# A fused two-block kernel on one core: another order of work in its first stage

## The chip, the cores and the metric

The kernel runs on one core of one Trainium2 chip. The metric is the device time of one execution in microseconds (us). Before the change it is 1601.06 us, the median of three runs (1599.04 to 1601.58).

## The reference

The input x has 512 rows of 1024 channels. Two blocks are computed in float32, cut here to what matters.

```python
def gated_deltanet_mixer(h, w_in, conv_w, a_log, dt_bias, o_gain, w_out):   # first mixer; h = rms_norm(x, a_norm)
    proj = h @ w_in                       # 4096 channels q,k,v; 2048 channels z; 16 channels "ab"
    qkv, z, ab = jnp.split(proj, [A_CONV_CH, A_CONV_CH + A_V_W], axis=-1)
    qkv = jax.nn.silu(causal_depthwise_conv(qkv, conv_w))                    # 4 taps
    q, k, v = ...                         # 8 heads; q and k are l2-normed
    beta = jax.nn.sigmoid(b_logit)
    g = -jnp.exp(a_log) * jax.nn.softplus(a_logit + dt_bias)                 # the gates, from the 16 channels
    o = chunk_gated_delta_rule(q, k, v, g, beta)                             # per head: a triangular solve, then a recurrence
    o = rms_norm(o, o_gain) * jax.nn.silu(z)
    return o @ w_out
```

After it come an attention with a sliding window, a second block with a pooling and a stick-breaking attention, an MLP and a gated embedding. The change touches nothing in those.

## The kernel before, in words

Everything is laid out with channels on the 128 partitions and the 512 rows of x along the free axis. The weights come as 214 blocks of 128x1024 (512 KB), each good for one group: 8 pieces, one for each 128 of the 1024 inner channels. A block passes from `wraw` (four buffers, loaded by the SP queue) to a high part `wh` (ACT, L1274) and a low part `wl` (DVE, L1867), both in the reduced float32 type; x is split in the same way into `XR[k]` and `XR[8+k]`. A piece is three matmuls of 512 columns, high x high, high x low and low x high (`mm3`), so a group is 24 matmuls into one PSUM bank. `walk` gives the order of a group's steps: OPEN (the blocks ahead are split), MM (one piece) with a STEP behind it, CLOSE (the eviction of a finished group) with a STEP. `Pace` says how many blocks are split ahead at each OPEN.

Each engine has its own program with the same parts, and `follow` runs them all in one order that is written by hand. `weave(g, order, parts, beside)` takes a plan such as "g10 g9 g17": it runs the next step of the named part (g, p, q, r) and then so many steps of the products. The engines keep to that order, each waiting on semaphores for what it needs.

The first stage goes so. `begin`: SP loads the eight tiles of x with the first weight blocks between them; ACT's queue loads gains, k1 (constants, among them the matrix of ones and the identity), wab (the gates' weights) and alog; POOL's queue loads the masks. ACT makes the high part of each tile of x times the gain (L1366), DVE the low part (L2064); then ACT squares the tiles (L1370) and DVE adds them up into `sqa` (L2070), clears `cin` (L2071) and splits the gates' weights (L2073). `products(1)` are the four groups of head 0, the first three side by side (`walk` with wide=3: for each piece k of x, one piece of each group), four groups of head 1 and six groups z. 24 steps of it run first. Then `rms_x` (ACT: logarithm and exponential of the sum of squares, L1379 and L1381, which give the row factor `rb_a`), 11 steps more, and then the gates with plan "a0": PE sums the squares over partitions with the matrix of ones and does the gates' product (24 matmuls with 16 weight columns); behind ten steps it transposes the scaled result (L898); behind nine more it does the product of gg with the triangle, for the running sum. DVE and ACT do the gates' short chain between (L2088 to L2102, L1394 to L1412). As the row factor is the same for all channels, it is applied when a group is evicted: for a head group DVE's multiplication into `cin` (L1917), then ACT's first tap of the convolution (L1302) and DVE's three others (L1903, the function `tap`). A z group has one eviction (L1922).

Plan "a1" then weaves `prep(0)` (part p) with the rest of `products(1)`. Its PE steps are the sum of k's squares (ks), G, kk, qk, the transposes kT, v0 and v1, all through one PSUM bank, so each waits until DVE or ACT has emptied it. Beside them DVE computes Dm, AT, qkT, kg and kd and the sums dc, then 15 shuffles of rows; POOL selects, masks, and inverts the 16x16 diagonal blocks in 15 turns of two instructions (L2611, L2613); DVE then writes U (L2183) and turns it into Tm (L2189). Plan "a2" weaves `prep(1)` (p), `levels(0)` (q), which starts with PE's product of Tm, and `recur(0)` (r) with the products of head 2 and z6.

Of the kernel before, what the change touches and what calls it, by code (L numbers as in the profile page):

```python
# [127 lines left out]
class Ring:  # L128


    def __init__(self, banks):
        self.use(banks)
# [118 lines left out]
def weave(g, order, parts, beside):  # L251
# [11 lines left out]

PLAN = {
    "a0": plan("g10 g9 g17"),
    "a1": plan("p5 p8 p2 p1 p2 p3 p10 p6 p6 p9 p6 p11 p14 p8"),
    "a2": plan("p2 p0 p0 q1 p2 q3 q1 p0 q5 q2 q0 p0 q2 p0 q3 r0 p1 r3 r1 r0 r1 p0 r1 r1 r4 p0 p1 r0 r2 p2 p5 p0 r1"),
# [20 lines left out]
def follow(p):  # L288
# [30 lines left out]
    def products(i):  # L319
        return chain(*(gemm(what, groups_of(what, h), 3 if (what, h) == ("head", 0) else 0, h) for what, h in PRODUCTS[i]))  # L320
# [3 lines left out]
    for _ in range(24):  # L324
        next(g)
    do("rms_x")
    for _ in range(11):
        next(g)
    banks(EARLY)
    weave(g, PLAN["a0"], {"g": part("gates")}, p.get("tap"))  # L330
    out = gemm("ao", pair_groups("wao", 8), 3, None, 2)
# [298 lines left out]
class Signals:  # L630


    def __init__(self, nc, ctx):
# [22 lines left out]

        self.gate_p, self.gate_a, self.gate_v = new("gate_pe"), new("gate_act"), new("gate_dve")
# [121 lines left out]
def tensor_program(e, m, s):  # L779
    p = {}  # L780
    ring = Ring(WIDE)
# [103 lines left out]
    def gates():  # L885
        e.wait_ge(s.k1, 16)
        e.wait_ge(s.xacc, 9)
        mm(m.banks[2][:], m.ones, m.sqa_a[:]).then_inc(s.nsum, 1)
        clear[2] = [(s.nln, 1)]
        e.wait_ge(s.gate_v, 1)  # L890
        for k, (xh, xl) in enumerate(m.pieces("head")):
            ins = mm3(m.banks[7][0:16, :], m.wabh[:, k, :], m.wabl[:, k, :], xh, xl, k == 0, k == 7)
        ins.then_inc(s.gate_p, 1)
        clear[7] = [(s.gate_v, 2)]
        yield
# [5 lines left out]
        clear[3] = [(s.gate_v, 3)]  # L901
        yield
# [351 lines left out]
def scalar_program(e, m, s):  # L1254
    p = {}
    ring, pace = Ring(WIDE), Pace()
# [96 lines left out]
    def begin():  # L1353
        e.dma_start(m.gains[:], m.d["gains"]).then_inc(s.gains, 16)
        e.dma_start(m.k1[:], m.d["k_k1"]).then_inc(s.k1, 16)
        e.dma_start(m.wab[:], m.d["wab"]).then_inc(s.wab, 16)
        e.dma_start(m.al[:], m.d["alog"]).then_inc(s.alog, 16)
        tables()
        for k in range(8):
            x = m.XF[:, 16 + k, :]  # L1360
            if k in (1, 2, 4):
                split(pace.upto(k // 2 + 1))
            e.wait_ge(s.x[k], 16)
            if k == 0:
                e.wait_ge(s.gains, 16)
            e.activation(m.XR[:, k, :], x, ACT.Copy, scale=m.gain("a_norm", k)).then_inc(s.xhi, 1)  # L1366
        for k in range(8):
            if k >= 2:
                e.wait_ge(s.xacc, k)
            e.activation(m.sqt_a[:, k % 2, :], m.XF[:, 16 + k, :], ACT.Square).then_inc(s.xsq, 1)  # L1370
        e.wait_ge(s.wab, 16)
        e.activation(m.wabh[:], m.wab[:], ACT.Copy).then_inc(s.gate_a, 1)
        passed["gate"] += 1
# [42 lines left out]
    def prep(h):  # L1416
# [43 lines left out]
        if h < 2:  # L1460
            e.wait_ge(s.xacc, 9)
        else:
            e.wait_ge(s.rec_v, REC_V * (h - 2) + 4)
# [383 lines left out]
def vector_program(e, m, s):  # L1847
    p = {}
    ring, pace = Ring(WIDE), Pace()
# [57 lines left out]
    def evac_head(n, bank, i, h):  # L1907
# [4 lines left out]
        if c == 0:  # L1912
            e.wait_ge(s.nrb, 1)
            e.wait_ge(s.xacc, 10)
# [144 lines left out]
    def begin():  # L2059
        for k in range(8):  # L2060
            if k in (1, 2, 4):
                split(pace.upto(k // 2 + 1))
# [3 lines left out]
        e.memset(m.sqa_a[:], 0.0).then_inc(s.xacc, 1)  # L2066
        for k in range(8):
            e.wait_ge(s.xsq, k + 1)
            e.wait_ge(s.xacc, k + 1)
            e.tensor_tensor(m.sqa_a[:], m.sqa_a[:], m.sqt_a[:, k % 2, :], ALU.add).then_inc(s.xacc, 1)  # L2070
        e.memset(m.cin[:], 0.0).then_inc(s.xacc, 1)  # L2071
        e.wait_ge(s.gate_a, 1)
        e.tensor_tensor(m.wabl[:], m.wab[:], m.wabh[:].bitcast(F), ALU.subtract).then_inc(s.gate_v, 1)  # L2073
        passed["gate"] += 1
# [447 lines left out]
def pool_program(e, m, s):  # L2522
# [13 lines left out]
    def begin():  # L2536
        e.dma_start(m.masks[:], m.d["k_masks"]).then_inc(s.masks, 16)
# [125 lines left out]
def sync_program(e, m, s):  # L2663
# [38 lines left out]
    def begin():  # L2702
# [4 lines left out]
        for k in (1, 2, 4):  # L2707
# [186 lines left out]
```

## Time and profile before

| | before |
|---|---|
| median of three runs | 1601.06 us |
| the profiled execution's own time | 1599.54 us |
| its span, first to last instruction | 1597.7 us |
| PE busy (matmuls) | 1548.9 us, 97% |
| DVE, ACT, POOL busy | 885.0, 747.5, 223.5 us |
| mean granted clock of TensorE | 0.995 |
| moved by DMA | 127.22 MB, mean 80 GB/s |

The profile is of one execution. PE is busy nearly all the time, so its idle time is the first thing to look for: the page shows the span in 40 slices of 40 us, one digit a slice, and PE's first two digits are 6 and 8, the others 9 save the last. The timeline is then read for the first 130 us, with the releaser of each wait in brackets behind a row.

### The profile page before, as it was taken

The numbers are of one execution on the slowest core, as the hardware profiler recorded it, in microseconds if no ns is written. First come the engines' busy times: TensorE is split into PE (matmuls) and PEld (weight loads), VectorE is DVE, ScalarE is ACT, GpSimd is POOL, SyncE is SP. The second block draws the span as 40 slices with busy tenths as digits, with TensorE's granted clock in tenths as the row PEclk, the third lists the DMA queues.
The fourth block names the chain that finished last, engine by engine and source line by source line (L and its number), as shares of the span: only waits on it lengthen the run. The fifth ranks groups of instructions, "written<-read, shape, count | busy, mean of one in ns | idle before, by whom it ended". The sixth has DMA issues, their size and how long they took to land.

```text
span 1597.7 us, 20673 instructions
## 1 busy us (share of the span) xinstructions
PE 1548.9 (97%) x7686; PEld 1228.5 (77%) x7686; DVE 885.0 (55%) x1633; ACT 747.5 (47%) x1293; POOL 223.5 (14%) x451
## 2 busy tenths in 40 slices
PE   6899999999999999999999999999999999999998
PEld 5688888888878767777777887666678888888876
DVE  4666777776666355555556435444366243443466
ACT  4453555544553346665567415555446232322333
POOL 1034224433323001221122000000000000000000
PEclk9999999999999999999999999999999999999999
DMA  4221111111114232222222232112122323232321
GB/s 185 80 84 49 54 58 63 53 54 59 48 53 150 81 106 81 85 67 80 67 86 67 80 105 75 53 53 66 53 80 80 106 93 106 93 105 87 98 81 65
DMA packets 40163, 127.22 MB, mean 80 GB/s; under 512 B 4576, under 2 KB 9104, under 8 KB 40064
## 3 DMA queue, kind: packets, MB, share of 16 engines
q1 hardware_dynamic: 38112, 121.65, 23.7%
q0 software_dynamic: 1040, 3.27, 0.6%
q8 instruction: 62, 1.02, 0.3%
q10 hardware_dynamic: 912, 0.99, 0.2%
q14 instruction: 37, 0.30, 0.1%
HBM read 122.69 MB, written 2.15 MB: 78 GB/s over the span
## 4 chain that ended last, share of the span: by engine, by line
PE 83%; DVE 7%; ACT 6%; issue 2%; DMA 1%; POOL 1%; SPq 0%; ACTq 0%; DVEq 0%; POOLq 0%
PE ps L792 81%; ACT L L1674 3%; DVE L L2353 1%; DVE wl L1867 1%; PE ps L1127 1%; DVE qkv L1903 1%; PE ps L919 1%; ACT wh L1274 1%; DMA wraw<-in_wa 1%; ACT L L1626 1%; DVE cin L1917 0%; DVE h L2488 0%; ACT xm L1809 0%; POOL masks L2611 0%; ACT qkv L1302 0%
## 5 line engine op out<-in xcount | busy, mean ns | idle before, releaser
L792 PE MATMUL ps<-xr,wh 128*128 128x512 f32 x2752 | 891.9, 405 | 15.1 <-DVE wl L1867 13.7
L792 PEld LDWEIGHTS ps<-xr,wh 128*128 128x128 f32 x2752 | 506.2, 189 | 144.6 <-issue 36.3
L792 PE MATMUL ps<-xr,wl 128*128 128x512 f32 x1376 | 540.0, 392 | 0.0
L1867 DVE TENSOR_TENSOR wl<-wraw,wh 128x1024 fp32r<-128x1024 f32 x214 | 262.0, 1230 | 157.7 <-ACT wh L1274 155.5
L792 PEld LDWEIGHTS ps<-xr,wl 128*128 128x128 f32 x1376 | 259.6, 189 | 56.2
L1274 ACT ACTIVATE wh<-wraw 128x1024 fp32r<-128x1024 f32 x214 | 221.8, 1049 | 81.9 <-PE ps L792 78.2
L792 PE MATMUL ps<-xm,wh 128*128 128x512 f32 x640 | 200.1, 394 | 6.7 <-DVE xm L2473 3.7
L792 PEld LDWEIGHTS ps<-xm,wh 128*128 128x128 f32 x640 | 120.3, 189 | 35.3 <-DVE xm L2473 5.0
L792 PE MATMUL ps<-xm,wl 128*128 128x512 f32 x320 | 125.1, 391 | 0.0
L2643 POOL TENSOR_SCALAR L<-L,m 128x256 f32<-128x256 f32 (+1 forms) x128 | 62.4, 510 | 315.5 <-DVE m L2368 315.5
L1903 DVE SCALAR_TENSOR_TENSOR qkv<-cin,gains,qkv 128x512 f32<-128x512 f32 x96 | 82.1, 855 | 11.1 <-ACT qkv L1302 10.3
L792 PEld LDWEIGHTS ps<-xm,wl 128*128 128x128 f32 x320 | 60.5, 189 | 12.6
L1674 ACT ACTIVATE L<-L,m 128x256 f32<-128x256 f32 (+1 forms) x128 | 59.9, 469 | 18.5 <-DVE m L2359 18.5
L1326 ACT ACTIVATE sqt<-sqt 128x512 f32<-128x512 f32 x32 | 20.2, 632 | 100.7 <-DVE sqt L2019 100.6
L1572 ACT ACTIVATE sqt<-h 128x512 f32<-128x512 f32 x24 | 14.9, 629 | 100.8 <-DVE h L1932 53.9
L2353 DVE CUSTOM_DVE_ANT_0 L<-ps,bias,sinks 128x256 f32<-128x256 f32 (+1 forms) x128 | 50.1, 447 | 13.9 <-PE ps L792 13.9
L2611 POOL TENSOR_TENSOR masks<-nb,uc 128x60 f32<-128x60 f32 (+14 forms) x120 | 44.1, 368 | 87.8 <-DVE nb L2173 72.1
L2038 DVE TENSOR_TENSOR mo<-ps,mo 128x512 f32<-128x512 f32 x24 | 16.6, 692 | 66.9 <-PE ps L792 66.9
L1694 ACT ACTIVATE pT<-ps 128x512 f32<-128x512 f32 x32 | 19.1, 597 | 71.1 <-PE ps L1127 71.1
L1302 ACT ACTIVATE qkv<-cin,gains 128x512 f32<-128x512 f32 x32 | 23.0, 723 | 50.1 <-DVE cin L1917 49.7
L2019 DVE SCALAR_TENSOR_TENSOR sqt<-ps,rb 128x512 f32<-128x512 f32 x32 | 22.0, 691 | 41.0 <-PE ps L792 36.0
L2613 POOL TENSOR_TENSOR uc<-uc,masks 128x60 f32<-128x60 f32 (+14 forms) x120 | 41.5, 346 | 9.4
(258 smaller groups left out, 1769.0 us busy)
## 6 DMA issues: line engine op xcount, KB each, us to landing
wraw<-in_wa SPq DMA_DIRECT2D x48, 512.0 KB, 3.7
wraw<-in_wb SPq DMA_DIRECT2D x32, 512.0 KB, 3.9
wraw<-in_wu SPq DMA_DIRECT2D x32, 512.0 KB, 3.7
wraw<-in_wd SPq DMA_DIRECT2D x32, 512.0 KB, 3.7
wraw<-in_wao SPq DMA_DIRECT2D x16, 512.0 KB, 3.7
wraw<-in_wbo SPq DMA_DIRECT2D x16, 512.0 KB, 4.0
wraw<-in_wc SPq DMA_DIRECT2D x16, 512.0 KB, 3.7
bias<-rel_rows SPq DMA_DIRECT2D x16, 256.0 KB, 3.9
```

The source lines that it names most:

```text
L792: return e.matmul(out, w, x, start=start, stop=stop, skip_group_check=True)
L1274: e.activation(m.wh[:, i % N_SPLIT, :], m.raw[:, i % N_RAW, :], ACT.Copy).then_inc(s.whi, 1)
L1302: e.activation(m.qkv[:, h % 2, n, :], m.cin[:, b, 3:515], ACT.Copy, scale=m.convw[:, 3, ch:ch + 1]).then_inc(s.conv0, 1)
L1326: e.activation(f, f, ACT.Square).then_inc(s.sq, 1)
L1674: e.activation(x, x, ACT.Exp, bias=m.nmx[:, c, u:u + 1], accum_out=m.den[:, c, u:u + 1]).then_inc(s.ex, 1)
L1867: e.tensor_tensor(m.wl[:, i % N_SPLIT, :], m.raw[:, i % N_RAW, :], m.wh[:, i % N_SPLIT, :].bitcast(F), ALU.subtract).then_inc(s.wlo, 1)
L1903: e.scalar_tensor_tensor(out=dst, in0=m.cin[:, c % 2, w:w + 512], scalar=m.convw[:, w, ch:ch + 1], in1=dst, op0=ALU.mult, op1=ALU.add).the ...
L2019: e.scalar_tensor_tensor(out=m.sqt[:, n % 2, :], in0=bank[:], scalar=0.0, in1=m.rb[:], op0=ALU.max, op1=ALU.mult).then_inc(s.relu, 1)
L2353: e.tensor_tensor_reduce(out=m.L[:, c, ee, n, lo:], in0=m.banks[4 + ee][:, 256 * (n % 2) + lo:256 * (n % 2) + 256], in1=m.bias[:, c, ee, lo:],
L2611: did(e.tensor_tensor(part, nb[:, :, r + 1:], m.uc[:, :, r:r + 1].to_broadcast([128, 4, w]), ALU.mult))
L2613: did(e.tensor_tensor(m.uc[:, :, r + 1:], m.uc[:, :, r + 1:], part, ALU.add))
L2643: e.tensor_scalar(x, x, m.den[:, c, 2 * n + ee:2 * n + ee + 1], 1.0, ALU.mult, ALU.mult).then_inc(s.pr, 1)
```

## The change

- Loads: k1 and alog are issued by ACT behind x's piece 4 (k counts from 0) and the split of block 2. The masks are issued by POOL once ACT has made five high parts of x.
- Order in `begin`: the splits of weight blocks 0, 1 and 2 stand behind x's pieces 0, 2 and 4 (before: ahead of pieces 1, 2 and 4, so behind 0, 1 and 3). The gates' weights are split at piece 0 instead of at the end. The sum of squares begins with a copy of the first square, not with a memset and an addition. `cin` is cleared by POOL at the very start.
- Head 0's first three groups still run side by side, but each now is two pieces behind the one before it (SKEW_X = 2), so there are 12 turns with one to three pieces each.
- The gates' product goes ahead of each of the first eight turns, a piece of three matmuls each time (`gates_x`). The sum of squares and the row factor (`rms_x`) come at turn 10. Plan "a0" goes from "g10 g9 g17" to "g52 g20 g14": the transposes come at once, the gates' chain on ACT and DVE 52 steps later, the product of gg 20 steps after that; the open taps are then all done (`flush`). Plans "a1" and "a2" are changed with it.
- PE begins with nine products of 128 columns on the cleared `cin`, whose result nobody reads.
- The order of the PSUM banks is (6, 0, 1, 4, 5) from the start.

```diff
     def __init__(self, banks):
-        self.use(banks)
+        self.banks, self.turn = banks, 0
     def use(self, banks):
...
+
+SKEW_X, RMS_AT, N_ZERO = 2, 10, 9
 PLAN = {
-    "a0": plan("g10 g9 g17"),
-    "a1": plan("p5 p8 p2 p1 p2 p3 p10 p6 p6 p9 p6 p11 p14 p8"),
-    "a2": plan("p2 p0 p0 q1 p2 q3 q1 p0 q5 q2 q0 p0 q2 p0 q3 r0 p1 r3 r1 r0 r1 p0 r1 r1 r4 p0 p1 r0 r2 p2 p5 p0 r1"),
+    "a0": plan("g52 g20 g14"),
+    "a1": plan("p1 p2 p2 p0 p2 p1 p1 p0 p1 p16 p14 p20 p10 p30"),
+    "a2": plan("p1 p4 p2 q0 p2 q4 q1 q2 q0 p0 q2 p0 q2 p0 q3 r0 p1 r0 r1 p0 r0 r2 r1 p0 r2 r0 r0 p4 r2 p0 p2 p0 r6"),
     "a8": plan("p0 q1 p2 q3 q1 q0 p0 q0 p3 q0 p0 q0 p0 q0 p1 r1 r0 r1 r0 p0 r0 p2 p0 r0 p0 r0 p2 r5 p0 r1 p0 r2 r1"),
...
     def products(i):
-        return chain(*(gemm(what, groups_of(what, h), 3 if (what, h) == ("head", 0) else 0, h) for what, h in PRODUCTS[i]))
+        return chain(*(gemm(what, groups_of(what, h), *((3, h, SKEW_X) if (what, h) == ("head", 0) else (0, h)))
+                       for what, h in PRODUCTS[i]))
...
     g = products(1)
-    for _ in range(24):
-        next(g)
-    do("rms_x")
-    for _ in range(11):
-        next(g)
-    banks(EARLY)
+    skew = SKEW_X
+    for t in range(8 + 2 * skew):
+        if t < 8:
+            do("gates_x", t)
+        drain(take(g, sum(0 <= t - skew * n < 8 for n in range(3))))
+        if t == RMS_AT:
+            do("rms_x")
     weave(g, PLAN["a0"], {"g": part("gates")}, p.get("tap"))
+    flush()
     out = gemm("ao", pair_groups("wao", 8), 3, None, 2)
...
+        self.cin = new("cin_cleared")
+
         self.gate_p, self.gate_a, self.gate_v = new("gate_pe"), new("gate_act"), new("gate_dve")
...
     p = {}
-    ring = Ring(WIDE)
+    ring = Ring(EARLY)
     p["banks"] = ring.use
...
     @part
-    def gates():
+    def begin():
+
+        e.wait_ge(s.cin, 1)
+        for _ in range(N_ZERO):
+            mm(m.banks[2][:, 0:128], m.cin[:, 0, 0:128], m.cin[:, 1, 0:128])
+
+    @part
+    def gates_x(k):
+
+        xh, xl = m.pieces("head")[k]
+        if k == 0:
+            e.wait_ge(s.gate_v, 1)
+        e.wait_ge(s.xlo, k + 1)
+        ins = mm3(m.banks[7][0:16, :], m.wabh[:, k, :], m.wabl[:, k, :], xh, xl, k == 0, k == 7)
+        if k == 7:
+            ins.then_inc(s.gate_p, 1)
+            clear[7] = [(s.gate_v, 2)]
+
+    @part
+    def rms_x():
         e.wait_ge(s.k1, 16)
-        e.wait_ge(s.xacc, 9)
+        e.wait_ge(s.xacc, 8)
         mm(m.banks[2][:], m.ones, m.sqa_a[:]).then_inc(s.nsum, 1)
         clear[2] = [(s.nln, 1)]
-        e.wait_ge(s.gate_v, 1)
-        for k, (xh, xl) in enumerate(m.pieces("head")):
-            ins = mm3(m.banks[7][0:16, :], m.wabh[:, k, :], m.wabl[:, k, :], xh, xl, k == 0, k == 7)
-        ins.then_inc(s.gate_p, 1)
-        clear[7] = [(s.gate_v, 2)]
-        yield
+
+    @part
+    def gates():
         e.wait_ge(s.gate_v, 2)
...
         clear[3] = [(s.gate_v, 3)]
+        yield
         yield
...
     p = {}
-    ring, pace = Ring(WIDE), Pace()
+    ring, pace = Ring(EARLY), Pace()
     p["banks"] = ring.use
...
     def begin():
         e.dma_start(m.gains[:], m.d["gains"]).then_inc(s.gains, 16)
-        e.dma_start(m.k1[:], m.d["k_k1"]).then_inc(s.k1, 16)
         e.dma_start(m.wab[:], m.d["wab"]).then_inc(s.wab, 16)
-        e.dma_start(m.al[:], m.d["alog"]).then_inc(s.alog, 16)
         tables()
         for k in range(8):
-            x = m.XF[:, 16 + k, :]
-            if k in (1, 2, 4):
-                split(pace.upto(k // 2 + 1))
             e.wait_ge(s.x[k], 16)
...
                 e.wait_ge(s.gains, 16)
-            e.activation(m.XR[:, k, :], x, ACT.Copy, scale=m.gain("a_norm", k)).then_inc(s.xhi, 1)
+            e.activation(m.XR[:, k, :], m.XF[:, 16 + k, :], ACT.Copy, scale=m.gain("a_norm", k)).then_inc(s.xhi, 1)
+            if k in (0, 2, 4):
+                split(pace.upto(k // 2 + 1))
+            if k == 0:
+                e.wait_ge(s.wab, 16)
+                e.activation(m.wabh[:], m.wab[:], ACT.Copy).then_inc(s.gate_a, 1)
+                passed["gate"] += 1
+            elif k == 4:
+                e.dma_start(m.k1[:], m.d["k_k1"]).then_inc(s.k1, 16)
+                e.dma_start(m.al[:], m.d["alog"]).then_inc(s.alog, 16)
         for k in range(8):
             if k >= 2:
-                e.wait_ge(s.xacc, k)
+                e.wait_ge(s.xacc, k - 1)
             e.activation(m.sqt_a[:, k % 2, :], m.XF[:, 16 + k, :], ACT.Square).then_inc(s.xsq, 1)
-        e.wait_ge(s.wab, 16)
-        e.activation(m.wabh[:], m.wab[:], ACT.Copy).then_inc(s.gate_a, 1)
-        passed["gate"] += 1
...
     def rms_x():
...
         if h < 2:
-            e.wait_ge(s.xacc, 9)
+            e.wait_ge(s.xacc, 8)
         else:
...
     p = {}
-    ring, pace = Ring(WIDE), Pace()
+    ring, pace = Ring(EARLY), Pace()
     p["banks"] = ring.use
...
             e.wait_ge(s.nrb, 1)
-            e.wait_ge(s.xacc, 10)
+            e.wait_ge(s.cin, 1)
         elif c >= 2:
...
     def begin():
         for k in range(8):
-            if k in (1, 2, 4):
-                split(pace.upto(k // 2 + 1))
             e.wait_ge(s.xhi, k + 1)
...
                                    in1=m.XR[:, k, :].bitcast(F), op0=ALU.mult, op1=ALU.subtract).then_inc(s.xlo, 1)
-        e.memset(m.sqa_a[:], 0.0).then_inc(s.xacc, 1)
+            if k in (0, 2, 4):
+                split(pace.upto(k // 2 + 1))
+            if k == 0:
+                e.wait_ge(s.gate_a, 1)
+                e.tensor_tensor(m.wabl[:], m.wab[:], m.wabh[:].bitcast(F), ALU.subtract).then_inc(s.gate_v, 1)
+                passed["gate"] += 1
         for k in range(8):
             e.wait_ge(s.xsq, k + 1)
-            e.wait_ge(s.xacc, k + 1)
-            e.tensor_tensor(m.sqa_a[:], m.sqa_a[:], m.sqt_a[:, k % 2, :], ALU.add).then_inc(s.xacc, 1)
-        e.memset(m.cin[:], 0.0).then_inc(s.xacc, 1)
-        e.wait_ge(s.gate_a, 1)
-        e.tensor_tensor(m.wabl[:], m.wab[:], m.wabh[:].bitcast(F), ALU.subtract).then_inc(s.gate_v, 1)
-        passed["gate"] += 1
+            if k == 0:
+                e.tensor_copy(m.sqa_a[:], m.sqt_a[:, 0, :]).then_inc(s.xacc, 1)
+            else:
+                e.wait_ge(s.xacc, k)
+                e.tensor_tensor(m.sqa_a[:], m.sqa_a[:], m.sqt_a[:, k % 2, :], ALU.add).then_inc(s.xacc, 1)
...
     def gates():
...
     def begin():
+        e.memset(m.cin[:], 0.0).then_inc(s.cin, 1)
+        e.wait_ge(s.xhi, 5)
         e.dma_start(m.masks[:], m.d["k_masks"]).then_inc(s.masks, 16)
...
                 load(k // 2 + 1)
-        for k in (1, 2, 4):
+        for k in (0, 2, 4):
             split(pace.upto(k // 2 + 1))
```

## Rows read from the trace of the kernel before

**Rows 1.** Waits of PE, 0 to 130 us: waiting <- releaser: total us, times, longest.

```profile
PE ps L792 <- DVE wl L1867: 12.4, 3, 9.0
```

**Rows 2.** Timeline of PE, 0 to 60 us: start, us, engine, line, operation, [idle before].

```profile
9.05 1.22 PE L792 MATMUL ps<-xr,wh 128*128 128x512 f32 x2 [9.05 <-DVE wl L1867]
...
13.09 1.22 PE L792 MATMUL ps<-xr,wh 128*128 128x512 f32 x2 [2.39 <-DVE wl L1867]
...
15.71 1.22 PE L792 MATMUL ps<-xr,wh 128*128 128x512 f32 x2 [0.98 <-DVE wl L1867]
...
19.50 0.63 PE L792 MATMUL ps<-xr,wh 128*128 128x512 f32 x2
...
37.21 0.62 PE L792 MATMUL ps<-xr,wh 128*128 128x512 f32 x2
```

**Rows 3.** Timeline of ACT and DVE, 0 to 60 us: the first pieces and the gates' weights.

```profile
4.10 0.72 ACT L1366 ACTIVATE xr<-xreg,gains 128x512 fp32r<-128x512 f32 x1 [0.18 <-DMA gains<-in_gains]
...
6.68 1.06 ACT L1274 ACTIVATE wh<-wraw 128x1024 fp32r<-128x1024 f32 x1 [1.86 <-DMA wraw<-in_wa]
...
7.77 1.23 DVE L1867 TENSOR_TENSOR wl<-wraw,wh 128x1024 fp32r<-128x1024 f32 x1 [2.16 <-ACT wh L1274]
...
24.43 0.30 ACT L1372 ACTIVATE wab<-wab 128x128 fp32r<-128x128 f32 x1
...
26.45 0.23 DVE L2073 TENSOR_TENSOR wab<-wab,wab 128x128 fp32r<-128x128 f32 x1
```

**Rows 4.** Windows (busy us by engine, PEclk, DMA share, GB/s), then DMA issues, 0 to 20.

```profile
0.00:10.00 10.00, 0.95 (x2) 0.84 (x3) 2.57 (x3) 3.78 (x4) 0.88 (x5) 1.00 0.83 304
...
masks<-in_k_masks POOLq DMA_DIRECT2D x1, 448.0 KB, 6.8
...
k<-in_k_k ACTq DMA_DIRECT2D x1, 420.0 KB, 6.5
```

**Rows 5.** Timeline, 20 to 60 us: the sum of squares, the factor, the gates' transposes.

```profile
37.90 1.02 PE L792 MATMUL ps<-sqa,k 128*128 128x512 f32 x2
...
39.74 0.63 ACT L1381 ACTIVATE rb<-rtmp 128x512 f32<-128x512 f32 x1
...
49.98 0.67 DVE L2088 TENSOR_TENSOR rtmp<-ps,rb 16x512 f32<-16x512 f32 x1
...
50.70 0.42 PE L898 MATMUL ps<-k,rtmp 16*128 16x16 f32 x4 [0.79 <-DVE rtmp L2088]
```

**Rows 6.** Timeline of DVE, 20 to 60 us: the weights' low part and two evictions.

```profile
48.83 1.23 DVE L1867 TENSOR_TENSOR wl<-wraw,wh 128x1024 fp32r<-128x1024 f32 x1 [1.74 <-ACT wh L1274]
...
52.99 0.69 DVE L1917 TENSOR_TENSOR cin<-ps,rb 128x512 f32<-128x512 f32 x1
...
58.99 0.69 DVE L1917 TENSOR_TENSOR cin<-ps,rb 128x512 f32<-128x512 f32 x1
```

**Rows 7.** Timeline of PE, 56 to 130 us: the wait for the gates and the products behind.

```profile
62.17 1.03 PE L792 MATMUL ps<-gg,k 128*128 128x32 f32 x4 [5.39 <-DVE gg L2102]
...
63.02 1.20 PE L792 MATMUL ps<-xr,wh 128*128 128x512 f32 x2
...
67.00 0.66 PE L792 MATMUL ps<-xr,wh 128*128 128x512 f32 x2
```

**Rows 8.** Timeline, 56 to 130 us, PE, DVE, POOL: head 0 from its norm to its levels.

```profile
76.83 1.10 PE L792 MATMUL ps<-rq,k 128*128 128x512 f32 x2 [0.76 <-ACT rq L1438]
...
95.24 0.68 DVE L2165 TENSOR_TENSOR kd<-ps,g 128x512 f32<-128x512 f32 x1
...
99.63 0.29 POOL L2611 TENSOR_TENSOR masks<-nb,uc 128x60 f32<-128x60 f32 x1 [7.59 <-DVE nb L2173]
...
113.03 0.21 POOL L2613 TENSOR_TENSOR uc<-uc,masks 128x4 f32<-128x4 f32 x1
...
116.30 0.71 DVE L2189 STREAM_TRANSPOSE Tm<-U 128x512 f32<-128x512 f32 x1
...
117.80 1.06 PE L792 MATMUL ps<-Tm,Mm 128*128 128x128 f32 x8
```


## The prediction

> **What bounds the kernel now.** I read the page first: PE is busy 97% of the span, and its low digits stand in the first slices. Then the waits of PE by stretch: between 0 and 130 us it waits 12.4 us for the weights' low parts in three pieces [rows 1], and further only for the four waits named below; the timeline shows no idle gap of PE between 77 and 260 us. So behind head 0's norm PE sets the pace, and any microsecond that PE gets back ahead of it, and doesn't lose again, comes off the end. The reader should make a ledger of what PE loses up to the first product of the levels (117.80 us) [rows 8]. A "piece" is three matmuls of 512 columns; at full pace 26 pieces run from 19.50 to 37.21 us, 0.681 us each [rows 2].
>
> The losses before: it starts at 9.05; it waits 2.39 and 0.98 for the second and third weight block; the first two lone pieces run at half pace (1.22 + 0.43, so 1.65 instead of 0.68: 1.94 together); from 15.71 to 19.50 three pieces take 3.79 instead of 2.04 (1.75) [rows 2]. It waits 0.79 for the gates' transposes [rows 5] and 5.39 for the gates (gg), behind which three pieces again run at half pace, 63.02 to 67.00, 3.98 instead of 2.04 (1.94) [rows 7]; and 0.76 for the squares of k [rows 8]. Sum 9.05 + 3.37 + 1.94 + 1.75 + 0.79 + 5.39 + 1.94 + 0.76 = **25.0 us**. The half pace is the 1.2 GHz level (512 columns in 0.43 us), though the window's granted clock reads 1.00 [rows 4]: here durations tell more than that column.
>
> **The start.** The DMAs are the limit: the window 0 to 10 has a DMA share of 0.83 at 304 GB/s, and in it land 448 KB of masks and 420 KB of k1 [rows 4], which go behind x. 868 KB at some 400 GB/s (the rate from 3 us on) are 2.2 us. x0's pass on ACT starts at 4.10 because of the table load and the gains [rows 3], and stays. Block 0 lands at 6.68 before; without k1 and masks ahead of it some 5.0. Then ACT's high part (1.06) ends 6.05, the gates' high part (0.30) 6.35, DVE's low part (1.23, from 6.05) 7.3, the gates' low part (0.23) **7.5** [rows 3]. There PE starts with the first gates product. New against before: the gates' product of each piece goes ahead of it, so PE has six pieces of work (7.5 to 11.6) before it asks for block 1, which is split by about 10.1, and block 2 is split by 12.8 when PE asks at 15. The skew of two pieces does that: no wait for blocks 1 and 2 (3.37 saved, and the lone pieces too). The gates' 24 products are not new work: they move from behind the sum. The squares go behind all of x: 5 us of ACT and 6 of DVE, done at about 21.5; the sum asks for them at 28.6, 7 us of cover. x's last low part comes at 14.8 instead of 18.3, asked for later still. k1 and alog now cost ACT two issues in mid stream (0.9 us, ahead of x5), which DVE, itself behind with low parts, hides; if x5 were late, PE would have 3 us to spare.
>
> **The products of zeros.** Nine f32 products of 128 columns, behind a memset of cin that goes to POOL. No row has either. A 512-column f32 product is 1.10 us at full pace [rows 8], so 0.28 for 128 columns, 0.55 at half: nine are 2.5 to 4.9 us. POOL starts about 1.3 and needs about a microsecond (DVE takes 0.92), so they end between 5 and 7.2, before 7.5: nothing in their own right. What they may give is the clock: the pace rose 3.8 us after 15.71 and 4.8 after 62.17 [rows 2, 7], and four microseconds of zeros are about that. I take full pace at 7.5 (idle gaps of 0.8 us left it at full, [rows 5, 8], one of 5.39 didn't, [rows 7]; the gap here is 0.5 to 2); the other end is 1.75 to 1.94 us. The Trainium skill, "TensorE: Matmul & The Clock Gate", Part 1, says that the chip watches how busy the array was, and that the number of slow matmuls differs between runs of one kernel; by that this term is not the same in all executions. No run here shows it for zeros.
>
> **The factor's wait.** From 7.5, 32 pieces and the sum (0.95) last until 30.25. The sum is issued at 28.6 with one piece behind it, then PE's transposes wait for the factor and the gates' scaling. Before: the sum is issued at 37.90, the factor done at 40.37, the scaling 0.67 on DVE, transposes 0.05 later [rows 5]: 3.25 us; so transposes at 31.85, and PE waits **1.6** (0.79 before).
>
> **The gates' wait.** The gg product now stands 72 steps behind the transposes (9 before), and its chain on ACT and DVE begins 52 steps behind them: 5.39 and the 1.94 of slow pieces behind it go, and nothing follows, since ACT and DVE need some 3 us and have 12.
>
> **Weight blocks in the first stage.** For the head groups the chain low part, three taps, eviction, first conv product on ACT, high part, low part is serial: evictions start 6.00 us apart (52.99, 58.99) [rows 6], while PE needs 8 x 0.681 = 5.45 per block. Before, the gates' wait paid for that. Now block 5 is split 9.7 us behind the factor (40.37 to 50.06) [rows 5, 6]: 31.1 + 9.7 = 40.8, block 10 five turns later at 70.8; PE asks for it at 32.2 + 7 x 5.47 = 70.4. Loss **0.4**; the earlier blocks are just in time. If PE started sooner, this chain would be late instead: it caps the gain.
>
> **Head 0 with less beside it.** 110 steps of the products now lie ahead of its norm instead of 71, so only 14 pieces are left beside it (49 before). PE: norm's sum at 83.4, then G, kk, qk, kT, v0, v1 through one bank with 3, 2, 1, 1, 1, 0 pieces between. G 86.4, kk 88.7, qk 90.4 and kT 92.1 wait 0.1 each at most. v0 waits for kd: kT ends 92.55, DVE has a low part (1.23) and kg, kd (0.68 each) [rows 6, 8] from 92.05: 94.65, PE there at 93.2: **1.4**. v1 waits for ACT's copy of v0: **0.65**. Then six pieces, head 1's norm sum, five pieces, and G of head 1 behind ACT's chain (two table loads, six silu and square passes, a weight block): about **0.55**. The levels wait for head 0's inversion on POOL: first shuffle 95.6. Before, POOL's steps ran from 99.63 to 113.24 (13.6 us, with a hole and three long ones beside DVE work), and DVE's two passes ended at 117.01 [rows 8]. With the shuffles in one go and DVE quiet I take 12 (ends: 10.9, 13.6) plus 1.5: 109.4. PE is there at 107.5: **1.9** (0.8 to 3.5).
>
> **The sum.** Losses after: 7.5 + 1.6 + 0.4 + 0.2 + 1.4 + 0.65 + 0.55 + 1.9 = 14.2. Gain 25.0 - 14.2 = 10.8. Cross-check by the levels' first product: before 117.80 with 114 pieces done, after 109.45 with 119 done: 117.80 + 3.4 - 109.45 = 11.7. I take 11.2. From there on nothing is changed but the order in head 1's stage, which I cost at nothing (bounds -1.5 and +2: PE doesn't wait between 118 and 260 now, so it can hardly gain). Against the profiled execution's 1599.54 that is 1588.3; the median of the runs is 1601.06, which gives 1589.9. I forecast **1589.0**.
>
> **The rivals.** (a) *The zeros don't raise the clock*, or it falls before 7.5: for it, no row shows f32 zeros at work and the gap up to 2 us; against it, the two times of rise. 1.75 to 1.94 more: 1591. (b) *The head 0 chain hides better than I wrote*: POOL in 10.9 us, PE's waits for kd and v0 shorter; up to 4 us less loss, 1585.5. Against it: kg, kd really stand behind a low part on DVE in both orders. (c) *The new orders expose more*: DVE stands in front of the inversion with head 2's weights and evictions queued behind it; only two blocks are split ahead. Waits of 3 to 6 us: 1594. (d) *Slower, one mechanism*: the chain from head 0's norm to the levels keeps the length that it has now, 76.83 to 117.80, 41 us [rows 8], since it is paced by engines and not by PE's order. PE has between the two only 21 pieces and some 7 us of f32 products, 21.4 us: it idles 19.6, and with 7.5 + 1.6 + 0.4 loses 29.1 against 25.0: 4 us slower, 1603.5. It decides from a chain of 37 us. Against it: 51 pieces of PE filled that chain, and the sum of its passes is 26 us. (e) *k1 and masks behind x don't speed block 0*, since the queues share the engines otherwise: start at 8.5 to 9, 1.0 to 1.5 more, 1590.3.
>
> **How the numbers follow.** The forecast with (e), 1587 to 1591: 0.55. (a) alone or with (e), 1591 to 1593: 0.14. (b) 1584 to 1587: 0.15. (c) 1593 to 1597.8: 0.11. No change: 0.03; (d): 0.02. The range 1584.5 to 1593.5 leaves out some 0.17. A difference under 0.2% (3.2 us) is about what a measurement of this kernel can't tell from none. Faster 0.94, same 0.04, slower 0.02.
>
> **What would show it.** Right: PE's first piece of x at 7.3 to 7.7, no wait for a low part until block 10; no PE wait for gg; waits of 1 to 2 us before the transposes, before v0 and before the first product of the levels; that product at about 109.5. The first gates products at 0.23 us each say that the zeros did their work, at 0.43 that they didn't. Wrong if PE waits over 4 us for the inversion, if evictions in the first stage are more than 6 us apart, or if later stages lose time that they don't lose now.

## The result and the profile after

The changed kernel takes 1593.01 us (median of four runs, 1590.44 to 1593.72), the kernel before 1600.59 beside it. The ratio is 0.9951, 95% interval 0.9933 to 0.9968: 0.5% or 7.8 us faster. The profiled execution took 1593.67 us, its span is 1591.9 us (before 1597.7).

The waits of PE from 0 to 130 us after the change (waiting <- releaser: total, times, longest):

```profile
PE ps L799 <- DVE wab L2093: 2.4, 1, 2.4
PE ps L799 <- POOL cin L2564: 1.8, 1, 1.8
PE ps L799 <- DVE Tm L2216: 1.5, 1, 1.5
PE ps L921 <- DVE rtmp L2115: 1.5, 1, 1.5
PE ps L943 <- DVE kd L2192: 1.1, 1, 1.1
PE ps L943 <- ACT vt L1497: 0.8, 1, 0.8
PE ps L799 <- ACT rq L1472: 0.5, 1, 0.5
PE ps L799 <- DVE AT L2180: 0.2, 1, 0.2
```

Before the change PE waited 9.0 us for the first low part and 5.4 us for gg [rows 1, 7]; neither wait is in this list. In their place stand eight shorter waits. Those for `cin` (1.8) and for the gates' weights (2.4) lie ahead of the first product of x, with the zeros between them, so the start on x itself moved by 0.7 us only. Lines are 7 to 29 higher than before: L799 answers to L792, L921 to L898, L943 to L919.

The timeline of PE, ACT, DVE and POOL at the places of rows 2 to 8 (start, duration, engine, line, operation, [idle before]):

```profile
1.75 4.21 PE L799 MATMUL ps<-cin 128*128 128x128 f32 x18 [1.75 <-POOL cin L2564]
...
8.37 1.46 PE L799 MATMUL ps<-xr,wab 128*16 128x512 f32 x3 [2.41 <-DVE wab L2093]
...
5.80 1.06 ACT L1298 ACTIVATE wh<-wraw 128x1024 fp32r<-128x1024 f32 x1 [0.99 <-DMA wraw<-in_wa]
...
30.93 1.02 PE L799 MATMUL ps<-sqa,k 128*128 128x512 f32 x2
...
34.16 0.42 PE L921 MATMUL ps<-k,rtmp 16*128 16x16 f32 x4 [1.51 <-DVE rtmp L2115]
...
34.51 0.80 PE L799 MATMUL ps<-xr,wh 128*128 128x512 f32 x2
...
38.96 0.62 PE L799 MATMUL ps<-xr,wh 128*128 128x512 f32 x2
...
51.42 0.69 DVE L1942 TENSOR_TENSOR cin<-ps,rb 128x512 f32<-128x512 f32 x1
...
57.42 0.69 DVE L1942 TENSOR_TENSOR cin<-ps,rb 128x512 f32<-128x512 f32 x1
...
98.91 0.63 PE L943 MATMUL ps<-k,qkv 128*128 128x128 f32 x4 [1.06 <-DVE kd L2192]
...
100.03 0.29 POOL L2640 TENSOR_TENSOR masks<-nb,uc 128x60 f32<-128x60 f32 x1 [4.00 <-DVE nb L2200]
...
111.08 0.21 POOL L2642 TENSOR_TENSOR uc<-uc,masks 128x4 f32<-128x4 f32 x1
...
113.88 1.16 PE L799 MATMUL ps<-Tm,Mm 128*128 128x128 f32 x8 [1.52 <-DVE Tm L2216]
```

PE works on zeros from 1.75 to 5.96 and on x from 8.37 (9.05 before) [rows 2]. Block 0 lands at 5.80 (6.68) [rows 3]. The sum is issued at 30.93 (37.90), the transposes come at 34.16 (50.70) after 1.51 us of idle time (0.79) [rows 5]. Head evictions are 6.00 us apart, as before [rows 6]. POOL's inversion takes 11.3 us (13.6) [rows 8].

The first product of the levels starts at 113.88 us with 119 pieces done; before at 117.80 with 114 [rows 8]. With 3.4 us for the five pieces that is a lead of 7.3 us. At the end of the span 5.8 are left of it. The other 1.5 us weren't lost in the changed stage: the lead fell by 1.5 at 583 us and by some 0.5 near the end, in code that the change doesn't touch, and rose by 0.4 at 451 us, where the kernel before has one slow piece. The waits and their lengths there are the same; what differs is the clock. The windows after, around the transposes and at 583 us (busy us of PE, PEld, DVE, ACT, POOL; granted clock; DMA share; GB/s), the product of PE that follows a wait there, and then the same place before:

```profile
34.50:38.10 3.60, 3.60 (x12) 2.80 (x11) 3.37 (x5) 1.33 (x2) 0.00 (x0) 0.57 0.37 127
...
583.00:588.00 5.00, 4.70 (x12) 3.43 (x13) 1.89 (x2) 2.52 (x4) 0.00 (x0) 0.66 0.80 210
```

```profile
583.30 1.10 PE L799 MATMUL ps<-L,k 128*128 128x512 f32 x2 [2.29 <-ACT L L1651]
```

```profile
589.00:594.00 5.00, 3.05 (x12) 2.22 (x13) 1.58 (x3) 2.51 (x4) 0.00 (x0) 1.00 0.82 177
```

```profile
590.95 1.10 PE L792 MATMUL ps<-L,k 128*128 128x512 f32 x2 [2.29 <-ACT L L1626]
```

The wait is 2.29 us in both kernels. Behind it the granted clock stayed at 1.00 in one execution and was 0.66 on the mean of the window in the other; the low product of a piece then lasts 0.63 us instead of 0.39. By the low products of 512 columns, stretches at the lower rate of two or three pieces each stand in the execution of before at 14, 64 and 1187 us; in the one of after, behind the start, at 35, 584, 1183 and 1544. Each costs 1.0 to 1.9 us, and which waits are followed by one changes from execution to execution. A second profiled execution of the changed kernel had none at 584 us: it was 0.7 us ahead of this one at 404 us and 2.2 ahead at 590, and its span is 2.3 shorter (1589.6). So one such stretch, there or not, makes about half of the spread of some 3 us between runs of one kernel.

### The profile page after: what moved, and what is told of

The parts are those of the page before. It is cut to its first block, busy times and chain, and to the rows that moved or that the text cites. A ratio compares the mean times of both kernels' runs of the same rounds, so it can differ in the third digit from the quotient of the medians.

```text
span 1591.9 us, 20708 instructions
## 1 busy us (share of the span) xinstructions
PE 1552.6 (98%) x7704; PEld 1231.2 (77%) x7704; DVE 885.2 (56%) x1631; ACT 748.0 (47%) x1293; POOL 221.6 (14%) x452
## 4 chain that ended last, share of the span: by engine, by line
PE 85%; DVE 6%; ACT 6%; issue 2%; POOL 1%; DMA 0%; ACTq 0%; POOLq 0%; SPq 0%; DVEq 0%
PE ps L799 83%; ACT L L1699 3%; DVE L L2380 1%; PE ps L1151 1%; DVE wl L1892 1%; PE ps L943 1%; ACT L L1651 1%; POOL uc L2642 0%; POOL masks L2640 0%; DVE U L2210 0%; ACT wh L1298 0%; DVE qkv L1928 0%; DMA wraw<-in_wa 0%; DVE h L2515 0%; DVE nb L2200 0%
## 5 line engine op out<-in xcount | busy, mean ns | idle before, releaser
L799 PE MATMUL ps<-xr,wh 128*128 128x512 f32 x2752 | 890.7, 405 | 2.9 <-DVE wl L1892 1.3
L799 PEld LDWEIGHTS ps<-xr,wh 128*128 128x128 f32 x2752 | 506.0, 189 | 132.6 <-issue 37.4
L799 PE MATMUL ps<-xr,wl 128*128 128x512 f32 x1376 | 539.8, 392 | 0.0
L799 PEld LDWEIGHTS ps<-xr,wl 128*128 128x128 f32 x1376 | 258.9, 188 | 56.0
L799 PE MATMUL ps<-xm,wh 128*128 128x512 f32 x640 | 201.0, 396 | 5.8 <-DVE xm L2502 3.0
L799 PEld LDWEIGHTS ps<-xm,wh 128*128 128x128 f32 x640 | 121.1, 190 | 34.3 <-DVE xm L2502 4.5
L799 PE MATMUL ps<-xm,wl 128*128 128x512 f32 x320 | 125.9, 393 | 0.0
L799 PEld LDWEIGHTS ps<-xm,wl 128*128 128x128 f32 x320 | 60.8, 190 | 12.9
L2640 POOL TENSOR_TENSOR masks<-nb,uc 128x60 f32<-128x60 f32 (+14 forms) x120 | 40.6, 338 | 80.7 <-DVE nb L2200 64.2
```

What stands on the lines that cost most here:

```text
L799: return e.matmul(out, w, x, start=start, stop=stop, skip_group_check=True)
L2640: did(e.tensor_tensor(part, nb[:, :, r + 1:], m.uc[:, :, r:r + 1].to_broadcast([128, 4, w]), ALU.mult))
```

## The experiments

Each was timed beside the kernel before. Its median there was 1599.44 us for the first four below; 1599.53 for constants early, no skew, the first timing of the old plans and the norm earlier; 1599.31 for the late constants alone and for the second timing of the changed kernel and the old plans. The ratio of each run is to those. Differences to the changed kernel are between medians of different timings. By the ratios they can be 1 to 2 us off: the changed kernel had 0.9951 (0.9933 to 0.9968) and, timed again, 0.9961 (0.9947 to 0.9974).

**Without zeros.**

```diff
-SKEW_X, RMS_AT, N_ZERO = 2, 10, 9
+SKEW_X, RMS_AT, N_ZERO = 2, 10, 0
```

> The changed kernel without the nine products of zeros. Theory A (in the changed kernel the zeros ran at half pace from 1.75 to 5.96 us and the first three turns of x at half pace again, 3.35 us for three pieces instead of 2.04, so they gave little): start of the first product of x at 8.4 as before, excess of the first pieces 1.8 to 1.9 us instead of 1.31, the time 0.5 us longer, within 0.1% of the changed kernel. Rival B (the zeros shortened the slow stretch by much more in most executions, and the profiled one was an unlucky one): 1.5 to 2 us longer by the median.

Measured 1592.98 us (1592.32 to 1593.78), ratio 0.9957 (0.9940 to 0.9973). PE starts on x at 8.22, and the sum is issued at 31.32, 0.4 later than with the zeros. The levels start at 114.13 (113.88 with the zeros). The nine products of zeros are worth nothing that can be measured: theory A.

**Sixteen zeros.**

```diff
+SKEW_X, RMS_AT, N_ZERO = 2, 10, 16
```

> Sixteen products of zeros instead of nine. Theory A (nine end at 5.96, and in the 2.4 us until the gates' weights come the clock isn't at its upper level; zeros up to the first product would bring it there): the rate of the zeros doubles at about 5.5 to 6, they end at 7.5 to 8, and the first products of x run at 0.22 to 0.25 us each: 1.3 us less than the changed kernel. Rival B (zeros don't count as work for the clock): all sixteen at 0.47 us each, end at 9.2, start of x's products 0.9 later and still at half pace: 0.9 us more than the changed kernel.

Measured 1591.54 (1591.38 to 1592.77), ratio 0.9948 (0.9933 to 0.9962), 1.5 less than the changed kernel. PE's timeline:

```profile
1.75 5.17 PE L799 MATMUL ps<-cin 128*128 128x128 f32 x32 [1.75 <-POOL cin L2564]
...
9.13 0.86 PE L799 MATMUL ps<-xr,wab 128*16 128x512 f32 x3 [2.20 <-DVE wab L2093]
```

32 instructions (two for each product) take 5.17 us, 0.16 each on the mean, where 18 took 4.21, 0.23 each. After 2.20 us of idle time the first gates piece takes 0.86 instead of 1.46. So products of zeros can raise the clock. With sixteen of them that piece took 0.86 to 0.88 in three traces of three, with nine in one of seven; without them it took 1.44. The Trainium skill, "TensorE: Matmul & The Clock Gate", Part 1, says that the clock is set by how busy the array has been lately; these traces agree. Theory A for the clock. The time is less clear: block 0 landed at 6.56 us here (5.80 in the changed kernel's profile), PE started on x 0.76 later, and the levels start at 113.32, 0.56 sooner and not 1.3. The 1.5 by the medians is near what can be told.

**The sum at turn 8.**

```diff
+SKEW_X, RMS_AT, N_ZERO = 2, 8, 9
```

> The sum of squares and the row factor at turn 8 of the first stage instead of turn 10, so that four pieces stand between the sum and the transposes instead of one. Theory A (the 1.51 us wait before the transposes in the changed kernel let the clock fall, and the three pieces behind it cost 1.73 us more): no wait, no slow pieces behind the transposes, 3.2 us less than the changed kernel at the first product of the levels and at the end; the serial chain of weight blocks (6.00 us each) is just in time for block 10. Rival B (the clock falls by the small transposes themselves, not by the wait): only the wait goes, 1.5 us less. Rival C (the block chain takes it back): PE waits for low parts of blocks 9 or 10, less than 1 us gained.

Measured 1590.00 (1589.00 to 1592.85), ratio 0.9939 (0.9924 to 0.9954), 3.0 less than the changed kernel. The sum and the transposes:

```profile
29.15 1.02 PE L799 MATMUL ps<-sqa,k 128*128 128x512 f32 x2
...
32.83 0.42 PE L921 MATMUL ps<-k,rtmp 16*128 16x16 f32 x4
...
111.08 1.16 PE L799 MATMUL ps<-Tm,Mm 128*128 128x128 f32 x8 [1.52 <-DVE Tm L2216]
```

There is no idle time before the transposes and no slow piece behind them, and the levels start 2.8 us sooner (3.2 were expected). By the ratios the gain on the changed kernel is 1.9 or 3.5 us, and the intervals overlap; the trace shows more clearly where it comes from. With the sum at turn 10 that wait is 1.5 us in each of the seven traces that have it (the changed kernel twice, without zeros, with sixteen, constants early, old plans twice), and in six of them two or three slow pieces follow (not in the first trace of the old plans). Here and in the three other runs with four pieces behind the sum (both edits, no skew, the norm earlier) the same transposes stand without the wait and nothing follows. Theory A; rival B falls, and so does C: no wait for a low part.

**Both.**

```diff
+SKEW_X, RMS_AT, N_ZERO = 2, 8, 16
```

> Both edits together: sixteen products of zeros and the sum at turn 8. Theory A: the two gains add up less what the block chain (6.00 us a block against PE's 5.45) takes back, since both the sum and PE move forward by the same: 4.5 us less than the changed kernel, about 1588. Rival C (PE is then in front of the block chain): as e3 alone, with waits for low parts of about a microsecond before block 10.

Measured 1587.89 (1587.81 to 1589.44), ratio 0.9925 (0.9911 to 0.9940), 5.1 less than the changed kernel. PE's first gates piece, its first product of the levels, and the window 28 to 40 us:

```profile
8.63 0.86 PE L799 MATMUL ps<-xr,wab 128*16 128x512 f32 x3 [0.17 <-DVE wab L2093]
...
109.64 1.16 PE L799 MATMUL ps<-Tm,Mm 128*128 128x128 f32 x8 [0.47 <-DVE Tm L2216]
```

```profile
28.00:40.00 12.00, 12.00 (x54) 9.33 (x53) 7.23 (x10) 5.28 (x7) 0.00 (x0) 1.00 0.13 44
```

PE has no idle time from 8.63 us until head 0's preparation, and the granted clock is 1.00 around the transposes. The gain is theory A's (4.5 expected), and of the four runs this is the only one that lies below all runs of the changed kernel; its interval overlaps with that of the changed kernel's first timing by 0.0007 and lies below that of the second. The first product of the levels starts at 109.64; the prediction had 109.45 for the change itself.

**Constants early.** k1 and alog back to ACT's first issues, the masks to POOL's.

```diff
         e.dma_start(m.gains[:], m.d["gains"]).then_inc(s.gains, 16)
+        e.dma_start(m.k1[:], m.d["k_k1"]).then_inc(s.k1, 16)
         e.dma_start(m.wab[:], m.d["wab"]).then_inc(s.wab, 16)
+        e.dma_start(m.al[:], m.d["alog"]).then_inc(s.alog, 16)
...
-        e.wait_ge(s.xhi, 5)
         e.dma_start(m.masks[:], m.d["k_masks"]).then_inc(s.masks, 16)
```

> The changed kernel with k1, alog and the masks issued at the very start again, everything else as changed. Theory A (DMA is the limit of the first 6 us, so 868 KB ahead of block 0 cost it time): weight block 0 lands at 6.7 instead of 5.80 us, the first product of x starts at 9.2 to 9.3 instead of 8.37, and behind it PE has enough work in hand not to wait for blocks 1 and 2: 0.9 us more. Rival B (the later pieces are held up as well): waits for low parts or for x behind the start, 2 us or more. Rival C (block 0 wasn't held up by them): no change, within 0.3 us at the start.

Measured 1595.09 (1593.63 to 1595.27, eight runs), ratio 0.9970 (0.9960 to 0.9981), 2.1 more than the changed kernel. ACT and PE at the start:

```profile
9.22 0.31 ACT L1392 ACTIVATE wab<-wab 128x128 fp32r<-128x128 f32 x1 [1.64 <-DMA wab<-in_wab]
...
9.91 1.46 PE L799 MATMUL ps<-xr,wab 128*16 128x512 f32 x3 [4.00 <-DVE wab L2092]
```

Block 0 lands at 6.52, near the theory's 6.7, but PE starts 1.54 later than in the changed kernel, not 0.9: the gates' weights are now what it waits for. They stand behind k1 in ACT's queue, and ACT waits for them until 9.22. Behind the start PE doesn't wait for blocks 1 and 2. Theory A with that term added. For block 0 alone it is weaker than it looks: in the eleven traces with the constants behind x, block 0 lands between 5.43 and 6.56, so 6.52 here and 6.68 in the kernel before stand at the edge of that spread. Block 2 shows the delay clearly: 13.34 and 13.52 with the constants early, 10.92 to 12.51 with them late.

**The late constants alone**, in the kernel before:

```diff
-        e.dma_start(m.k1[:], m.d["k_k1"]).then_inc(s.k1, 16)
-        e.dma_start(m.al[:], m.d["alog"]).then_inc(s.alog, 16)
...
+            if k == 4:
+                e.dma_start(m.k1[:], m.d["k_k1"]).then_inc(s.k1, 16)
+                e.dma_start(m.al[:], m.d["alog"]).then_inc(s.alog, 16)
...
+        e.wait_ge(s.xhi, 5)
         e.dma_start(m.masks[:], m.d["k_masks"]).then_inc(s.masks, 16)
```

> The kernel before with one part of the change alone: k1 and alog issued by ACT behind x's piece 4, the masks by POOL behind ACT's five high parts. Theory A (the first blocks come as fast as the 868 KB ahead of them let them): block 0 lands at 5.8 instead of 6.68, blocks 1 and 2 some 2.2 us sooner, the products of the three groups start at 8.2, 11.0 and 13.5 instead of 9.05, 13.09 and 15.71, and the whole is 2.2 us shorter, since sum, factor and the block chain all move with it: ratio 0.9986. Rival B (what the start gives is taken back by the gates' wait, which hangs on the serial chain of weight blocks): the wait for gg grows by as much, no change at the first product of the levels.

Measured 1598.33 (1596.93 to 1599.07, ten runs), ratio 0.9991 (0.9982 to 1.0000). PE's first product of each block, and of gg:

```profile
8.08 1.22 PE L792 MATMUL ps<-xr,wh 128*128 128x512 f32 x2 [8.08 <-DVE wl L1868]
...
10.96 1.22 PE L792 MATMUL ps<-xr,wh 128*128 128x512 f32 x2 [1.23 <-DVE wl L1868]
...
13.60 1.22 PE L792 MATMUL ps<-xr,wh 128*128 128x512 f32 x2 [0.99 <-DVE wl L1868]
...
59.96 1.03 PE L792 MATMUL ps<-gg,k 128*128 128x32 f32 x4 [5.36 <-DVE gg L2103]
```

The three starts are those expected within 0.15 us, the wait for gg is 5.36 as before (5.39), and the levels' first product comes at 115.55 against 117.80 [rows 8]: the 2.2 us stay to there (A). The timed ratio gives 1.4 us, with an interval from 0 to 2.9, so the time by itself doesn't settle it.

**No skew.**

```diff
+SKEW_X, RMS_AT, N_ZERO = 0, 6, 9
```

> The first head's three groups level again (no skew: three pieces a turn, eight turns), the sum at turn 6 so that four pieces stand behind it as in the run with the sum at turn 8, all else as changed. Theory A (the skew gives PE work of group 0 while blocks 1 and 2 come): a wait of about 1.8 us for block 2's low part (ready at 13.5, asked for at 11.7) and maybe a shorter one for block 1: 1.5 to 2 us more than the run with the sum at turn 8, by the median 1591.5 to 1592. Rival B (the gates' pieces ahead of each turn are cover enough): no wait, the same time as that run.

Measured 1593.02 (1591.55 to 1594.62), ratio 0.9961 (0.9946 to 0.9976), 3.0 more than with the sum at turn 8 and skew 2. PE asks for blocks 1 and 2:

```profile
11.90 0.73 PE L799 MATMUL ps<-xr,wh 128*128 128x512 f32 x2 [0.78 <-DVE wl L1892]
...
14.55 0.90 PE L799 MATMUL ps<-xr,wh 128*128 128x512 f32 x2 [1.69 <-DVE wl L1892]
```

There are two waits, of 2.5 us together, where about 1.8 and perhaps a shorter one were expected (A). The transposes come 4.3 us later than in the run with the sum at turn 8 (37.09 against 32.83): behind the second wait three more pieces run at the lower rate, up to 18 us, which costs 1.6.

**The old plans.** a1 and a2 as before, a0 with the gates' product 30 steps behind the transposes.

```diff
-    "a0": plan("g52 g20 g14"),
+    "a0": plan("g21 g9 g17"),
```

> The changed kernel with the plans of before for a1 and a2, and a0 as g21 g9 g17, so that the product of gg stands 30 steps behind the transposes as near as before in the sequence, and head 0's norm has about 50 pieces beside it again. Theory A (the later gates are worth the 5.39 us wait for gg and the slow pieces behind it, less the 4 us of waits in head 0's preparation that they bring): a wait for gg of 2 to 5 us and slow pieces behind it, no waits for kd, vt and Tm; 1.5 to 3 us more than the changed kernel. Rival B (the waits for kd, vt and Tm cost as much as the gates' wait did): the same time within 1 us.

> The changed kernel once more, beside the next one. In the traces the changed kernel is 2.1 us ahead of the one with the old plans at the first product of the levels (113.8 with 119 pieces done against 112.6 with 114). Theory A (that lead stays to the end): it is 1.5 to 2.5 us faster than the next one. Rival B (the lead is lost in the later head stages): the same within 0.7 us.

> The old plans for a0, a1 and a2 in the changed kernel once more, beside the one before. Theory A: 1.5 to 2.5 us slower than it. Rival B: the same within 0.7 us.

Measured 1592.69 (1592.00 to 1593.71), ratio 0.9959 (0.9945 to 0.9973). Timed once more side by side: the changed kernel 1593.16 (1591.40 to 1594.54), 0.9961 (0.9947 to 0.9974); the old plans 1592.55 (1592.31 to 1594.93), 0.9958 (0.9946 to 0.9971). Rival B in both: the same. From the first trace of the old plans, gg, G of head 0 and the first product of the levels; from the second, gg and the norm's sum:

```profile
55.55 1.03 PE L799 MATMUL ps<-gg,k 128*128 128x32 f32 x4 [3.50 <-DVE gg L2129]
...
79.97 1.13 PE L799 MATMUL ps<-k,gg 128*128 128x128 f32 x8 [1.31 <-ACT rq L1472]
...
112.57 1.06 PE L799 MATMUL ps<-Tm,Mm 128*128 128x128 f32 x8
```

```profile
53.18 0.60 PE L799 MATMUL ps<-gg,k 128*128 128x32 f32 x4 [1.86 <-DVE gg L2129]
...
67.66 1.10 PE L799 MATMUL ps<-rq,k 128*128 128x512 f32 x2 [1.27 <-ACT rq L1463]
```

The wait for gg is 3.50 or 1.86 us instead of 5.39, and head 0's preparation waits 1.5 or 2.6 us for ACT. The waits for kd, vt and Tm (3.3 us) are not there. In the first trace the changed kernel is 2.1 us ahead at the levels; in the second (110.21 with 114 pieces against 113.95 with 119) it is 0.3 behind. A slow stretch more or less on either side decides that.

**The norm earlier**, on top of the run with both edits.

```diff
-    "a0": plan("g52 g20 g14"),
-    "a1": plan("p1 p2 p2 p0 p2 p1 p1 p0 p1 p16 p14 p20 p10 p30"),
+    "a0": plan("g44 g16 g17"),
+    "a1": plan("p1 p2 p2 p0 p2 p1 p3 p1 p1 p16 p14 p20 p10 p30"),
```

> Sixteen zeros and the sum at turn 8, and the plans a0 g44 g16 g17 and a1 p1 p2 p2 p0 p2 p1 p3 p1 p1 p16: head 0's norm nine steps earlier, three pieces between the transposes of k and v0 and one between v0 and v1. Theory A (the waits for kd 1.1, vt 0.8, Tm 0.5 are a matter of how many pieces stand between): kd's wait gone, vt's down to 0.2, Tm's gone, 2 to 2.3 us less than the run with sixteen zeros and the sum at turn 8, about 1585.7; head 1's weight block chain 0.5 us longer for the gates' chain inside it. Rival B (ACT comes too late with head 0's squares, being behind the weight blocks): a wait for the squares of k of 1 to 3 us takes it back.

Measured 1586.78 (1586.05 to 1587.46), ratio 0.9922 (0.9907 to 0.9936): 13 us less than before, the fastest kernel of this study; 1.1 less than the run with both edits, where 2 to 2.3 were expected, and the intervals don't part the two. The waits for kd, vt and Tm are gone, as A has it, and the levels' first product starts at 108.14, 1.5 us sooner, with the same 119 pieces done. But PE now meets the chain of weight blocks:

```profile
72.10 0.70 PE L799 MATMUL ps<-xr,wh 128*128 128x512 f32 x2 [1.28 <-DVE wl L1892]
```

It waits 1.28 us for block 10, since the gates' short chain stands inside one turn of that chain (the evictions at 60.37 and 68.30 are 7.9 us apart, not 6.0), and 0.74 in two waits for ACT. That the block chain becomes the next bound is what the prediction said of an earlier start.

## Why the prediction was right or wrong

The forecast was 1589.0 with 1584.5 to 1593.5; measured 1593.0. The sign and nearly every wait were right. The gain of 11.2 was 7.6 by the medians, so the number lies only 0.5 us inside the slow end of the range. By the terms of its sum (losses of PE up to the levels):

| term | predicted | measured |
|---|---|---|
| start on x | 7.5 | 8.37 |
| slow first pieces | 0 (up to 1.9) | 1.31 |
| wait before the transposes | 1.6 | 1.51 |
| slow pieces behind that wait | not in the sum | 1.73 |
| block 10 | 0.4 | 0 |
| small waits, kd, vt | 0.2, 1.4, 0.65 | 0.2, 1.06, 0.78 |
| G of head 1 | 0.55 | 0.46 |
| first product of the levels | 1.9 | 1.52 |
| sum | 14.2 | 16.9 |

The losses came out 2.7 us larger than predicted: 3.0 by the clock and 0.9 by the start, less 1.2 by the rest, which is luck and not foresight. The ledger gives a gain of 25.0 - 16.9 = 8.1 where the start of the levels gives 7.3: 0.8 us stand in none of its terms. Two small slips don't matter to the result: the way from the sum to the transposes is 3.19 us by the prediction's own rows, not 3.25 (measured 3.23), and 95.6 + 12 + 1.5 is 109.1, not 109.4. **The clock is what failed.** The first part of it (1.31) is rival (a), to which I gave 0.14: the step "I take full pace at 7.5" took nine zeros for enough. That this term would differ between executions held: with nine zeros one trace of seven starts at full pace. The second part (1.73) has no place in the prediction at all: the step "The factor's wait" priced the wait before the transposes at its length, 1.6, although the wait for gg in its own ledger stood with the slow pieces behind it [rows 7]. The rows had a wait of 0.79 without that price and one of 5.39 with it [rows 5, 7]; 1.6 lay between, and neither end was taken into the range. With the sum two turns earlier the wait and its slow pieces go (3.0 us by the medians, 2.8 in the trace); with sixteen zeros the slow first pieces go (1.5 by the medians). With both the kernel comes within 0.2 us of the predicted start of the levels, and its median is 1587.9. That this is the forecast's 1588.3 is chance: this run has no wait before the transposes and 0.47 before the levels, where the forecast has 1.6 and 1.9, and starts 1.1 later.

**The start** was mis-sized by 0.87. Block 0 landed 0.9 earlier than before where I had 1.7, and in none of the eleven traces with late constants did it land before 5.43. I had priced most of the 868 KB as ahead of it; x's next pieces, issued from 1.66 us on, were in flight as well, but no run separates the two. The 2.2 us that I had for the 868 KB came out at blocks 1 and 2, which landed 2.1 sooner with the late constants alone. That the gates' weights would have been the later arrival, had k1 stayed ahead of them, I didn't see; it is half of the 1.54 us by which the run with early constants starts later.

**Block 10** made no wait because PE was 4 us later than predicted; evictions are 6.00 us apart as forecast. In the run with both edits PE is there at 70.2 us (70.4 predicted) and the block's low part is ready at 70.05, just in time; in the run with the norm earlier the wait came, 1.28 us.

**The gates' wait** was booked as 7.3 us saved with 4.7 of new waits in head 0's preparation. Taken by itself the change of the plans is worth nothing that can be measured. The waits that it brings were right in the sum within 0.7 us; what wasn't is the saving. With the old plans the product of gg still stands behind 48 pieces, as before the change, but everything ahead of it comes sooner (gg is ready at 55.40 or 53.03 us instead of 62.03), and the wait for it shrinks to 3.5 or 1.9 by itself. Terms that were each right against the kernel before were booked to a part that doesn't own them.

**Rivals.** (d) is refuted: from head 0's norm sum to the levels it took 26.8 us (87.10 to 113.88), not 41; the prediction said 26. (c) didn't come: behind the levels the lead went from 7.3 to 7.1 us until 153 us and stayed between 6.8 and 7.7 until 583. (b): the waits for kd and Tm were 0.3 to 0.4 shorter, no more. (e) is refuted for blocks 1 and 2 by the run with the late constants alone; for block 0 it is not far off: PE started at 8.37, nearer to its 8.5 than to my 7.5.

What stays open: why the wait of 1.5 us before the transposes was followed by a slow stretch in six traces of seven, while the longer ones at 583 and 1543 us were in some only, and one of 1.54 us near 600 us was in none of thirteen. No run here moved one wait by itself and left its length. That the wait is the cause and not the transposes rests on the four runs that have them without it.

## What to carry to other kernels

Price a wait of TensorE at its length plus what the pieces behind it may lose by the clock, here up to 1.9 us. The length alone doesn't tell when: the waits of 1.06 and 0.78 us for kd and vt were followed by two slow pieces in four of eight traces. There it cost nothing, since the wait before the levels shrank from 1.5 to about 0.5 us; with no such wait behind it, a slow stretch comes off the end. So put cover ahead of waits on the main engine's path first: moving the sum by two turns was worth about 3 us. Make a ledger against one kernel and then ask of each saving whether another part of the change would already have brought it. Where a serial chain over engines has a pitch (6.00 us here) near the main engine's (5.45), it is the next bound, and each gain before it has to be checked against it.

## What the runs showed of the hardware

- A wait of 2.29 us at the same place left the granted clock at 1.00 in one execution and took it down to a mean of 0.66 over the next 5 us in another.
- Block 0, a load of 512 KB issued at about 1.2 us, landed between 5.43 and 6.56 us in eleven traces with the same loads ahead of it.
- The eighteen instructions on zeros took between 3.68 us (no skew) and 4.21 us (changed kernel) in seven traces with the same start, so the clock rose at different points of them or not at all. Behind them and 2.0 to 4.0 us of idle time the first gates piece took 1.25 to 1.46 us six times and 0.88 once (the old plans' second trace). Sixteen products took 5.17 to 6.71 us, and behind them and 0.2 to 2.2 us of idle time it took 0.86 to 0.88 in three traces of three.
- Over the slow first pieces (8.3 to 11 us) the column of the granted clock read 1.00 in five traces (before, late constants alone, changed, no zeros, old plans) and 0.51, 0.66, 0.50 and 0.56 in four others (sum at turn 8, constants early, no skew, changed again), at the same durations. Over those behind the transposes it read 0.57. So at the start of this kernel the durations tell, not the column.
